# First expert group of an encoder layer: six of its sixteen value sums are placed among the transposes, queries and scores of tiles 2 and 3

## The reference, cut to what matters

```python
def peer_ffn(hn, w_q, sub_keys, u_emb, v_emb):        # blocks of 128 tokens
    q = (xc @ w_q).reshape(T, PEER_HEADS, 2, PEER_HALF)
    s = jnp.einsum('thsd,hsnd->thsn', q, sub_keys)
    s1, i1 = lax.top_k(s[:, :, 0], 16)
    s2, i2 = lax.top_k(s[:, :, 1], 16)
    cand_s = s1[..., :, None] + s2[..., None, :]      # 256 pairs
    top_s, pos = lax.top_k(cand_s, 16)
    idx = jnp.take_along_axis(cand_i, pos, axis=-1)
    gate = jax.nn.softmax(top_s, axis=-1)
    act = jax.nn.gelu(jnp.einsum('thkd,td->thk', u_emb[idx], xc))
    return jnp.einsum('thk,thkd->td', gate * act, v_emb[idx])
```

## Time and profile before

| | |
|---|---|
| median of 3 runs | 2082.99 us (2081.72 to 2086.61) |
| the profiled execution | 2079.8 us, span 2077.5 us |
| TensorE matmuls, busy share of the span | 86% |
| VectorE | 68% |
| ScalarE | 35% |
| GpSimd | 34% |
| DMA, mean over the span | 355 GB/s |
| chain that ended last | TensorE 44%, DMA 25%, VectorE 16%, issue 7% |

### The profile page before, as it was taken

How to read it: one execution, slowest core, us unless ns; L and a number is a source line. 1 busy time by engine, 2 the same in 40 slices (tenths; PEclk the granted TensorE clock), 3 DMA queues, 4 the chain that set the end, 5 groups by cost and what they waited for, 6 DMA issues and landing times.

```text
span 2077.5 us, 19311 instructions
## 1 busy us (share of the span) xinstructions
PE 1784.5 (86%) x5959; PEld 994.7 (48%) x5959; DVE 1421.3 (68%) x2951; ACT 734.3 (35%) x1949; POOL 709.5 (34%) x659
## 2 busy tenths in 40 slices
PE   5998899999999999899789879888969878987876
PEld 5656434787997675334334334333423333433332
DVE  5894775434453277887777787787677777777765
ACT  3344443222333234343243333333333433343333
POOL 6990000000000034354444444344444444444441
PEclk9998899999999999999989989989999999999999
DMA  9775999888999989999999999999999999999996
GB/s 263 206 197 128 249 294 274 263 249 263 306 282 327 305 323 388 417 421 421 417 421 421 417 421 421 418 421 421 417 418 421 415 408 414 414 418 418 421 414 263
DMA packets 199313, 737.24 MB, mean 355 GB/s; under 512 B 31222, under 2 KB 97963, under 8 KB 133675
## 3 DMA queue, kind: packets, MB, share of 16 engines
q0 software_dynamic: 74112, 537.95, 62.7%
q1 hardware_dynamic: 125098, 198.07, 32.1%
HBM read 731.78 MB, written 136.31 MB: 418 GB/s over the span
## 4 chain that ended last, share of the span: by engine, by line
PE 44%; DMA 25%; DVE 16%; issue 7%; POOL 4%; ACT 4%; SPq 0%; DVEq 0%; ACTq 0%; POOLq 0%
PE bank L1671 23%; PE bank L1958 17%; DMA R<-uv_rows,R 10%; DMA WS<-uv_rows,R 8%; DMA slabs<-uv_rows,R 6%; PE bank L1992 3%; DVE R L1535 2%; PE bank L1660 1%; POOL WS L2049 1%; POOL R L2049 1%; DVE R L1485 1%; DVE R L1488 1%; DVE R L1486 1%; DVE R L1516 1%; DVE R L1519 1%
## 5 line engine op out<-in xcount | busy, mean ns | idle before, releaser
L1958 PE MATMUL bank<-R 128*128 128x512 f32 x1368 | 675.7, 639 | 149.1 <-ACT R L1008 149.0
L2134 POOL DMA_INDIRECT R<-uv_rows,R x342 | 384.8, 1125 | 511.2 <-PE bank L1958 486.7
L1535 DVE CUSTOM_DVE_ANT_0 R<-R,XN 128x1024 f32<-128x1024 f32 x342 | 419.5, 1227 | 169.6 <-DMA R<-uv_rows,R 155.9
L1958 PEld LDWEIGHTS bank<-R 128*128 128x128 f32 x1368 | 272.5, 204 | 525.3 <-issue 311.5
L1001 ACT ACTIVATE R<-R 128x2 f32<-128x2 f32 (+1 forms) x257 | 52.1, 203 | 803.5 <-DVE R L1535 803.1
L2134 POOL DMA_INDIRECT WS<-uv_rows,R x86 | 95.6, 1112 | 687.4 <-DVEq L1522 587.0
L1671 PE MATMUL bank<-R 128*64 128x64 f32 (+6 forms) x776 | 186.0, 387 | 20.0 <-DVE R L1232 7.4
L1958 PE MATMUL bank<-slabs,R 128*128 128x512 f32 x336 | 164.2, 630 | 29.0 <-ACT R L1008 29.0
L1958 PE MATMUL bank<-WS,R 128*128 128x512 f32 x344 | 164.1, 617 | 25.8 <-ACT R L1008 25.8
L1008 ACT ACTIVATE R<-cst,R 128x128 f32<-128x128 f32 x512 | 177.7, 394 | 8.4
L1535 DVE CUSTOM_DVE_ANT_0 R<-WS,XN 128x1024 f32<-128x1024 f32 x86 | 105.4, 1226 | 45.2 <-DMA WS<-uv_rows,R 41.6
(11 more groups left out here) (228 smaller groups left out, 2157.3 us busy)
## 6 DMA issues: line engine op xcount, KB each, us to landing
uv_rows<-in_peer_u SPq DMA_DIRECT2D x8, 4096.0 KB, 23.6
uv_rows<-in_peer_v SPq DMA_DIRECT2D x8, 4096.0 KB, 35.3
uv_rows<-in_peer_v SPq DMA_DIRECT2D x10, 2048.0 KB, 13.3
uv_rows<-in_peer_u SPq DMA_DIRECT2D x9, 2048.0 KB, 14.0
uv_rows<-in_peer_u SPq DMA_DIRECT2D x11, 1024.0 KB, 8.2
slabs<-in_w_in SPq DMA_DIRECT2D x17, 512.0 KB, 5.3
slabs<-in_w_mem_kv SPq DMA_DIRECT2D x8, 1024.0 KB, 11.8
slabs<-in_w_peer_q SPq DMA_DIRECT2D x8, 1024.0 KB, 25.4
```

The costliest lines, as they stand in the source:

```text
L1535: dve.tensor_tensor_reduce(prod, rings[i % RING][:, 0:D], xn[:, t, :], 1.0, 0.0, ALU.mult, ALU.add, act_row[:, s:s + 1]).then_inc(dots, 1)
L1958: last = pe.matmul(ps[2 * (t % 2) + n][:, :], diag[s], v[:, D + 512 * n:D + 512 * n + 512], start=(s == 0), stop=(s == TOPK - 1))
L2134: pool.indirect_dma_start(out=rings[i % RING], out_offset=None, in_=UV, in_offset=bass.IndirectOffsetOnAxis(ap=idx[t][:, s:s + 1], axis=0) ...
```

## The change

The same instructions are issued; their order changes on TensorE, ScalarE and VectorE. On TensorE the sums of slots 10 and 11 stand between the turns and the queries, 12 and 13 between the two halves of the queries, 14 between the two halves of the scores, and 15 and the following ones behind them. ScalarE weighs slots 10 to 13 ahead of `later_features` (before: behind it). VectorE takes the dot products of slots 10 and 11 before it normalises tiles 2 and 3, and those of 12 and 13 before the gates of group 1. GpSimd's and SyncE's programs are unchanged.

```diff
@@ scalar
             await_full(act, ("mo", 3, 2))
             weigh(0, 4)
             squares(6, H, junk2, lambda n, t: ("mo", t, n))
-            later_features()
             weigh(0, 5)
             weigh(0, 6)
+            later_features()
             queries_out(0, 0, True)
             weigh(0, 7)
@@ vector
             mem_out((2, 2), (3, 2))
-            dot_products(0, 0, range(9, 10))
+            dot_products(0, 0, range(9, 12))
             normal_tiles(6, 2, 3)
+            dot_products(0, 0, range(12, 14))
             gates_of(1)
-            dot_products(0, 0, range(10, TOPK))
+            dot_products(0, 0, range(14, TOPK))
@@ tensor
                 turn(("pT", k), lambda b: [(b[:, columns(t)], xn[:, t, columns(k)]) for t in (2, 3)])
+            slots(0, 0, range(10, 12))
             for k in range(KD):
                 await_drained(pe, ("pT", k))
@@ tensor
             queries(0, 0, first=True)
+            slots(0, 0, range(12, 14))
             queries(0, 1, first=True)
-            slots(0, 0, range(10, 12))
             scores(0, 0, first=True)
+            slots(0, 0, range(14, 15))
             scores(0, 1, first=True)
-            slots(0, 0, range(12, TOPK))
+            slots(0, 0, range(15, TOPK))
             head(0, first=True)
```

## The result

| | before | changed |
|---|---|---|
| median of 13 runs each, on one chip | 2081.76 us | 2091.31 us |
| ratio, 95% interval | | 1.0038 [1.0028, 1.0049] |
| profiled execution, its span | 2079.8, 2077.5 us | 2088.9, 2086.6 us |
| first gather issued | 742.32 us | 742.75 us |
| first gather to end of span | 1335.2 us | 1343.8 us |

The prediction named 2090 us, with a range of 2082 to 2096, and 7.1 us more than before. The changed kernel is slower by 7.9 us by the ratio (5.8 to 10.2 by its interval), and its median lies 9.6 us higher. From the first gather on, the changed kernel takes 8.6 us more.

A forecast was written before the change was run, and what follows sets the result against it. From the first gather on, DMA engines bound the kernel: gather bytes plus moments without work. Hole -2.9, first gap +7.6, second place +2.4 make +7.1 us, named as 2090 us, range 2082 to 2096.

The forecast's parts named there:

- The hole, -2.9 us: DMA engines idle at 802 to 804 us; issuing gather 22 at 793.7 fills this and saves 2.9 us.
- TensorE's row of work and the clock: TensorE from the turns to slot 16 runs without pause, ending at 811.5; idle time before the queries had cost 1.9 us.
- The load and the stall: Head 1's query weights, loaded at 805.4 beside gathers, land at 823.7; TensorE waits 12.2 us behind slot 16; chance 0.66.
- The restart: After the stall TensorE loses 1.8 us at half rate; gather 29 issues at 828.4, lands at 833.8, +4.7 us.
- From slot 17 to slot 31, "no room to catch up": TensorE frees a gather each 2.58 us, DMA engines need 2.5: the delay is not won back and no backlog builds.
- The second place, 2.4 us: At gather 54, late indices from head 1's scores shift it +7.1 us, 2.4 us more than gather 53.
- The rule on the queues: Each DMA engine goes round robin between queues with work, changing only at packet boundaries; equal turns would give 1 MB in 5 us.
- about 1 us later, and the next gathers don't wait for it: VectorE gets head 0's scores at 808.0, about 1 us later; the next gathers don't wait for the resulting indices.

The follow-up runs named there:

- e6: Changed kernel with half of head 1's query-weight load issued early, queries in one piece and both scores ahead of slots 12 to 15; ratio to before 0.9995, repeated 0.9989.
- e5: Kernel before, order untouched, but SyncE also waits for the sum of slot 12 before loading head 1's query weights; ratio to before 1.0072.
- e1: Changed kernel with only slots 10 and 11 moved on TensorE; queries in one piece, slots 12 to 15 behind the scores; ratio to before 1.0024.
- e7: Kernel before, but from gather 48 on GpSimd allows at most two, three or five gathers in flight; one execution each took 2488.04, 2260.69 and 2080.65 us.
- e4: Changed kernel with head 1's query-weight load cut in two, the first half loaded early into a free buffer; ratio to before 1.0009.

## Why the prediction was right, step by step

**The hole, -2.9 us.** Right against the execution that it was read from. Gather 22 was to go out at 793.7 and did at 794.11, with a first gather 0.43 us later than in before; the ledger gives +3.1 by 65 us. But 1.5 to 1.6 of the 2.9 us came from the half clock of that one execution; in three of the five profiles with before's queries they were not there (see e6).

**TensorE's row of work and the clock.** Right: first queries at 795.39 (said 795.1), slot 16 at its end 811.9 (811.5). The clock stays at 1.00 until TensorE stops, where in before it fell to 0.55 after 2.37 us of idle time. That such an idle time always costs 1.9 us, as the prediction took it, is wrong: in e5 and in the kernels with two and five in flight it cost nothing.

**The load and the stall.** Right, to the half microsecond: issued at 805.93 (805.4), 18.3 us to its use (18.3), query of head 1 at 824.26 (823.7), a wait of 12.3 us (12.2). The estimate that all queued bytes end together held in the changed kernel. It is an estimate of the end, not of the share: in e1 and e5 it was 23.1 and 21.0 us from the load's issue to its use.

**The restart.** Right: clock 0.50 at 822 to 826 us, while TensorE still waits and in its first 2 us of work, gather 29 at 828.83 (828.4), landed after 5.4 us at 834.2 (5.4, 833.8). It lands 5.2 us later than in before, 4.8 net of the later start of the gathers (4.7).

**From slot 17 to slot 31, "no room to catch up".** Here the sum was short of a term. I had put the transfers at 2.5 us each, the rate of a full queue, and 0 us of loss; the ledger has 3.1. The rows of gathers 29 and 39 (issue in the form, then the time to landing):

```profile
L2137 POOL DMA_INDIRECT R<-uv_rows,R x1: 947/947/947, 828.8 to 828.8; - x1
...
DMA to landing us min/median/max: 5.4/5.4/5.4
...
L2137 POOL DMA_INDIRECT R<-uv_rows,R x1: 1862/1862/1862, 854.6 to 854.6; - x1
...
DMA to landing us min/median/max: 8.6/8.6/8.6
```

They land at 834.2 and 863.2, 2.9 us each, and the way from issue to landing grows: the gathers are issued faster than they are served. In before the same ten took 2.57 each (829.1 to 854.7). The shift grows from 5.2 to 8.5 us, with the clock of TensorE at 1.00 and its period at 2.57 us throughout. With 5.4 to 8.6 us to land and one issue each 2.57 us, two to three gathers are in flight there, and e7 shows that the rate is lower at such a depth (2.92 us each with three). What keeps the DMA engines busy without moving bytes at that rate, no run shows.

**The second place, 2.4 us.** The place is right, the mechanism only in part. Gather 54 goes out at 897.43 (said 896.7) and lands after 6.0 us, at 903.4. It was to land 2.4 us later than gather 53's own lateness explains. But gather 53 landed only at 901.0, 8.5 us later than in before, since the DMA engines were 8.4 us late by then and not 4.7, and gather 54 is late by no more than that, 8.4 us. The further loss of 1.5 us in the ledger falls right behind it, between 155 and 165 us. There TensorE's slots 42 and 43 took 6.43 us (before 5.25), and gather 55 went out 2.64 us behind gather 54 (before 1.72), 11.3 us later than in before:

```profile
893.37 6.43 PE L1959 MATMUL bank<-R 128*128 128x512 f32 x8 [3.78 <-ACT R L1008]
```

The terms added up: 4.7 + 2.4 = 7.1 us was said, and the ledger has 5.3 + 3.1 + 1.5 = 9.9, of which the drift after 700 us, whose cause is open, takes off 1.3, to 8.6. The one term that was missing (3.1 us) is partly made up for by the last one (-0.9) and by that drift; that 7.1 is so near to the 7.9 us of the ratio is partly luck. The interval of 5.8 to 10.2 us and the medians, 9.6 us apart, don't tell 7.1 from 9.9.

**The rule on the queues** ("DMA: Bandwidth & Descriptors" of the Trainium skill, section "Queues, rings and completion order") was used rightly with the row beside it. The turns are far from equal in bytes: no load of 1 MB beside gathers took the 5 us of equal turns. Behind the first, those of before took 25.1 to 26.6 us, and those of the kernel with three gathers in flight 13.7 to 24.1; the first one took 18.3 to its use in the changed kernel.

**What I did not say.** The rival that the interleaving delays VectorE was missing; "about 1 us later, and the next gathers don't wait for it" was true of the changed kernel, because the stall gave VectorE room: its dot product for slot 28 ended some 12 us before TensorE came to it. e4 showed that it is false as soon as the stall is gone.

## What to carry to other kernels

When a hole in the DMA engines' work is to be filled, look first at who uses it: a small transfer on another queue that lands in the hole in 5 us takes 18 to 27 beside a full stream of large ones, and a long wait may hang on it. Issue such a transfer one stage earlier, into any buffer that is free, before the hole is closed. And when one wait goes, ask which chain is the next one: here it was VectorE's search, and the order of the scores and three slots decided over 4 us. Before a gain of 1 or 2 us is believed, look whether the kernel before has the same wait or clock in each of its executions: here TensorE ran its queries at half clock in two of five, which made the hole 1.5 to 1.6 us larger.

## What the runs showed of the hardware

- A gather of 1.05 MB needs company: 309 GB/s with two in flight, 364 with three, 414 with five, 420 with the buffers all in use (the first three hold the way from a landing to the next issue too). A DMA share of 0.96 to 0.99 does not mean full rate; 355 to 371 GB/s went with it.
- What the stretch up to the first gather takes varies by up to 8 us between executions of nearly the same program (740.42 to 748.43 us). From the first gather on two profiles of one kernel, e6, agree at 1333.6 us. For a change of under 10 us the span from a fixed event tells more than the time of the whole, but it isn't free of scatter either.
- After the same idle time of TensorE, 2.3 to 2.4 us between the same instructions, the granted clock fell to 0.50 in two profiles (the queries took 8.83 us) and stayed at 1.00 in three (7.14 us).
